# Attention: the scaled gate of tiles 1 to 14 is turned by VectorE in blocks and placed through memory, no longer by TensorE

## The reference, cut to what matters

```python
z = jnp.einsum('btd,dc->btc', x, w_in)
q, k, v, g_attn, hq, hf, hi, g_hg = jnp.split(z, _split_points(), axis=-1)
...
attn = _sink_window_attend(qb, k2, v2, qpos, kpos, sk).reshape(B, T, ATTN_WIDTH)
...
attn = _rmsnorm(attn, attn_g) * jax.nn.silu(g_attn.astype(jnp.float32))
...
mix = jnp.einsum('btc,cd->btd', jnp.concatenate([attn, o_hg], axis=-1), w_out.astype(jnp.float32))
```

## Time and profile before

| | us |
|---|---|
| median of three runs | 2558.17 |
| the profiled execution | 2546.3 |
| its span, first to last instruction | 2544.5 |
| PE busy in it | 2493.5 (98%) |
| DVE busy | 1705.2 (67%) |
| POOL busy | 1172.3 (46%) |
| ACT busy | 1113.5 (44%) |
| mean granted PE clock, share of full | 0.998 |

### The profile page before, as it was taken

One profiled execution on the slowest core, in us unless ns is written; L12 is line 12 of the kernel. 1 busy time (PEld: TensorE's weight loads), 2 busy tenths in 40 slices (PEclk: granted clock), 3 DMA queues, 4 the chain that ended last, 5 costly groups with the idle time before them and its releaser, 6 DMA issues. The chain is left out here.

```text
span 2544.5 us, 55195 instructions
## 1 busy us (share of the span) xinstructions
PE 2493.5 (98%) x20706; PEld 2044.3 (80%) x20706; DVE 1705.2 (67%) x3230; ACT 1113.5 (44%) x2542; POOL 1172.3 (46%) x1119
## 2 busy tenths in 40 slices
PE   8999989999999999999999999899999999999998
PEld 6788868888888788888888788688888887887887
DVE  5777777777676676654557777776777676866343
ACT  4455465555555510133334454555555554112322
POOL 2234315555556611496322443165555555116863
PEclk9999999999999999999999999999999999999999
DMA  5445552011110488765734555510111005877532
GB/s 182 154 172 185 187 186 70 27 43 43 44 38 25 175 288 293 273 216 172 264 123 154 186 179 178 190 35 31 43 43 51 31 33 195 313 270 257 170 135 91
DMA packets 176099, 365.44 MB, mean 144 GB/s; under 512 B 19104, under 2 KB 98464, under 8 KB 170272
## 3 DMA queue, kind: packets, MB, share of 16 engines
q1 hardware_dynamic: 175504, 363.11, 41.6%
q10 hardware_dynamic: 432, 0.08, 0.0%
HBM read 227.14 MB, written 137.89 MB: 143 GB/s over the span
## 5 line engine op out<-in xcount | busy, mean ns | idle before, releaser
L1947 PE MATMUL r_Z<-w_rec_parts,w_rec_xh 128*128 128x512 f32 x1920 | 610.3, 399 | 1.8 <-DVE r_kT L1768 0.9
L1947 PEld LDWEIGHTS r_Z<-w_rec_parts,w_rec_xh 128*128 128x128 f32 x1920 | 347.7, 188 | 71.9 <-issue 3.5
L1947 PE MATMUL r_Z<-w_rec_parts,w_rec_xl 128*128 128x512 f32 x960 | 375.7, 391 | 0.0
L124 PE MATMUL a_Z<-w_attn_high,w_attn_xh 128*128 128x512 f32 (+1 forms) x816 | 302.3, 370 | 11.6 <-DVE w_attn_low L211 9.7
L124 PE MATMUL a_Z<-w_attn_low,w_attn_xh 128*128 128x512 f32 (+1 forms) x816 | 290.6, 356 | 0.0
L124 PE MATMUL a_Z<-w_attn_high,w_attn_xl 128*128 128x512 f32 (+1 forms) x816 | 290.3, 356 | 0.0
L1649 ACT ACTIVATE r_E<-r_E 128x512 f32<-128x512 f32 x230 | 145.3, 632 | 294.6 <-DVE r_E L1805 292.1
L1540 POOL TENSOR_TENSOR r_qE<-r_qT,r_E 128x256 f32<-128x256 f32 x230 | 185.1, 805 | 190.6 <-ACT r_E L1649 115.4
L1947 PEld LDWEIGHTS r_Z<-w_rec_parts,w_rec_xl 128*128 128x128 f32 x960 | 180.2, 188 | 39.7
L1540 POOL TENSOR_TENSOR r_kE<-r_kT,r_E 128x256 f32<-128x256 f32 x230 | 201.2, 875 | 0.0
L124 PEld LDWEIGHTS a_Z<-w_attn_high,w_attn_xh 128*128 128x128 f32 x816 | 154.8, 190 | 39.9 <-issue 19.3
(11 more groups left out here) (338 smaller groups left out, 6409.3 us busy)
## 6 DMA issues: line engine op xcount, KB each, us to landing
dram_h_rows<-o_hb SPq DMA_DIRECT2D x34, 512.0 KB, 4.1
o_raw<-dram_hT SPq DMA_DIRECT2D x34, 512.0 KB, 4.3
o_hb<-dram_h_rows SPq DMA_DIRECT2D x34, 512.0 KB, 3.8
dram_y_all<-o_hb SPq DMA_DIRECT2D x34, 512.0 KB, 4.1
w_attn_xraw<-dram_xT SPq DMA_DIRECT2D x33, 512.0 KB, 5.7
w_rec_slot<-dram_w_in SPq DMA_DIRECT2D x16, 1024.0 KB, 8.2
o_mraw<-dram_mixT SPq DMA_DIRECT2D x32, 512.0 KB, 5.6
dram_hT<-o_hT SPq DMA_DIRECT2D x128, 128.0 KB, 2.6
```

What stands on the lines that cost most here:

```text
L124: mm = pe.matmul(out, a[:, c, :], b[:, c, :], start=(first and c == chunks[0] and a is xh and b is wh), stop=(last and c == chunks[-1] and ...
L1947: mm = pe.matmul(banks[what], x[:, c, :], w[:, cols[what]], start=(c == 0 and x is xh[k] and w is wh[c]), stop=(c == KC - 1 and x is xl[k]))
```

## The change

DVE no longer waits for PE with the gate. For tiles 1 to 14 `scale_gate` moves ahead of `row_max`; behind it a new `turn_gate` transposes `u` by blocks of 32x32 into `th`, the buffer of the gate's tanh. SP's new `store_gate` writes `th` to memory in four transfers (32 partitions each), and `load_gate_turned` reads it back into `attn`, now transposed as a whole. `gated` multiplies `attnT` by `attn` instead of by `T`, and it moves behind `unfold`. PE's `transpose_gate` goes from the step; `values` now waits for `ms_done` instead of `uT_out`. `gate_tanh` waits until the gate of two tiles earlier is back, since it writes `th`. Tiles 0, 15 and 16 keep the transposition on PE. The memory used is the one that the output phase writes later, and the semaphores of its transfers are renamed (`hT_st` to `turned_st`, `h_in` to `turned_in`); nothing else changes there.

```diff
@@ SP
+            def gate_home(n):
+                return dram["hT"][layer, n][:, 0:AW]
+
+            def store_gate(j, k):
+                n = 2 * j + k
+                sp.wait_ge(*S["turned"].at(n))
+                for i in range(4):
+                    sp.dma_start(gate_home(n).rearrange("(q r) (i x) -> i r q x", q=4, i=4)[i],
+                                 th[32 * i:32 * i + 32, :].rearrange("r (q x) -> r q x", q=4))                        .then_inc((S["turned_st0"], S["turned_st1"])[k].sem, 16)
+
+            def load_gate_turned(j, k):
+                n = 2 * j + k
+                sp.wait_ge(*(S["turned_st0"], S["turned_st1"])[k].at(64 * (j + k)))
+                sp.wait_ge(*S["uT_out"].at(n))
+                sp.dma_start(attn[:, :], gate_home(n)).then_inc(S["turned_in"].sem, 16)
...
             for j in range(1, PAIRS - 1):
                 c = 4 * (j - 1)
+                store_gate(j, 0)
                 exchange_part(c)
+                load_gate_turned(j, 0)
                 store_mix(j - 1, 1)
                 load_x(j + 2, 0)
                 exchange_part(c + 1)
                 store_mix(j, 0)
+                store_gate(j, 1)
                 exchange_part(c + 2)
+                load_gate_turned(j, 1)
@@ ACT, gate_tanh
                 wait(act, S["gate_done"], n)
+                if not isinstance(n, int) or n > 2:
+                    act.wait_ge(*S["turned_in"].at(16 * (n - 2)))
@@ DVE
             def scale_gate(j, k):
...
-                wait(dve, S["gT_ps"], n)
+                if isinstance(n, int) and n in (1, NT - 1):
+                    dve.wait_ge(*S["gT_ps"].at(1 if n == 1 else 2))
                 dve.tensor_scalar(u[:, :].rearrange("p (i s d) -> p s i d", s=KV, d=HD),
                                   gate[k][:, :].rearrange("p (s i d) -> p s i d", s=KV, d=HD), rstd[:, 0:1], None,
                                   ALU.mult).then_inc(S["scaled"].sem, 1)
 
+            def turn_gate(j, k):
+                n = 2 * j + k
+                dve.wait_ge(*S["scaled"].at(n + 1))
+                dve.transpose(th[:, :].rearrange("p (q i t) -> p q i t", q=4, i=4),
+                              u[:, :].rearrange("p (i q t) -> p q i t", q=4, i=4)).then_inc(S["turned"].sem, 1)
+
             def gated(j, k):
                 n = 2 * j + k
-                dve.wait_ge(*S["gT_ps"].at(n + 1))
+                if by_transfer(n):
+                    dve.wait_ge(*S["turned_in"].at(16 * n))
+                    wait(dve, S["attnT_done"], n)
+                    wait(dve, (S["mix_st0"], S["mix_st1"])[k], 64 * j)
+                    dve.tensor_tensor(in_tokens(mixT[k][:, :, :]), in_tokens(attnT[:, :, :]),
+                                      attn[:, :].rearrange("p (i c t) -> p c i t", i=4, c=4), ALU.mult)                        .then_inc(S["uT_out"].sem, 1)
+                    return
...
             def step(j, k, *chunks):
                 sum_squares(j - 1 + k, 1 - k)
+                scale_gate(j - 1 + k, 1 - k)
+                turn_gate(j - 1 + k, 1 - k)
                 row_max(j, k)
-                scale_gate(j - 1 + k, 1 - k)
                 for c in chunks[0:1]:
                     low_part(c, 2 * (1 - k))
                 divide(j, k)
                 rope(j + k, 1 - k)
+                unfold(j, k)
                 gated(j - 1 + k, 1 - k)
-                unfold(j, k)
                 gates(j + k, 1 - k)
@@ PE
             def values(j, k):
                 n = 2 * j + k
                 wait(pe, S["unfolded"], KV * n)
                 pe.wait_ge(*S["v_moved"].at(n + 1))
-                wait(pe, S["uT_out"], n)
+                if isinstance(n, int) and n in (1, NT - 1):
+                    pe.wait_ge(*S["uT_out"].at(n))
+                else:
+                    pe.wait_ge(*S["ms_done"].at(n))
...
                 score(j, k)
                 z_q(j + k, 1 - k)
-                transpose_gate(j - 1 + k, 1 - k)
                 z_g(j + k, 1 - k, 0)
```

More of the change, by code:

```diff
@@ L152 @@
     **counted(NT, "m_high m_split mix_ps summed stats_done var_done ve_done rstd_done scaled h_done"),
-    **counted(16 * NT, "m_in row_in h_in rows_in p_in"), "ln_in": 32, "weights_read": 2,
+    **counted(16 * NT, "m_in row_in turned_in rows_in p_in"), "ln_in": 32, "weights_read": 2,
     **counted(16 * (PAIRS + 1), "h_st0 y_st0"), **counted(16 * PAIRS, "h_st1 y_st1"),
-    **counted(64 * (PAIRS + 1), "hT_st0 yT_st0"), **counted(64 * PAIRS, "hT_st1 yT_st1"),
+    **counted(64 * (PAIRS + 1), "turned_st0 yT_st0"), **counted(64 * PAIRS, "turned_st1 yT_st1"),
     **counted(NT, "p_high p_split ple_ps blend y_done"), "turned": 2 * NT,
@@ L530, in attention_phase, with by_transfer @@
         own, before = slice(P, 2 * P), slice(0, P)
+        def by_transfer(n):
+            return not isinstance(n, int) or 1 <= n <= NT - 3
         part = [weights.beside[n][:, :] for n in ("part0", "part1")] + [kcT[:, :, :].rearrange("p b d -> p (b d)")]
@@ L651, in _ @@
             load_x(2, 1)
+            store_gate(0, 1)
+            load_gate_turned(0, 1)
             for j in range(1, PAIRS - 1):
                 c = 4 * (j - 1)
+                store_gate(j, 0)
                 exchange_part(c)
+                load_gate_turned(j, 0)
                 store_mix(j - 1, 1)
@@ L667, in _ @@
             store_mix(PAIRS - 2, 1)
+            store_gate(PAIRS - 1, 0)
+            load_gate_turned(PAIRS - 1, 0)
             sp.wait_ge(*S["z_g"].at(NT))
@@ L1035, in scale_gate @@
                                   ALU.mult).then_inc(S["scaled"].sem, 1)
+            def turn_gate(j, k):
[3 more added lines that the diff above has]
+                              u[:, :].rearrange("p (i q t) -> p q i t", q=4, i=4)).then_inc(S["turned"].sem, 1)
             def gated(j, k):
                 n = 2 * j + k
-                dve.wait_ge(*S["gT_ps"].at(n + 1))
+                if by_transfer(n):
[5 more added lines that the diff above has]
+                    return
+                dve.wait_ge(*S["gT_ps"].at(2 if n == NT - 2 else 3))
                 wait(dve, S["attnT_done"], n)
@@ L2205, in output_phase @@
         K = (slice(0, KC // 2), slice(KC // 2, KC))
-        h_st, hT_st = (S["h_st0"], S["h_st1"]), (S["hT_st0"], S["hT_st1"])
+        h_st, turned_st = (S["h_st0"], S["h_st1"]), (S["turned_st0"], S["turned_st1"])
         y_st, yT_st = (S["y_st0"], S["y_st1"]), (S["yT_st0"], S["yT_st1"])
@@ L2239, in store_h @@
                 for to, of in turned_to(th[0] if n == NT - 1 else hT[k], dram["hT"][layer, n]):
-                    sp.dma_start(to, of).then_inc(hT_st[k].sem, 16)
+                    sp.dma_start(to, of).then_inc(turned_st[k].sem, 16)
             def load_h(n, made):
                 k = n % 2
-                sp.wait_ge(*hT_st[k].at(64 * (n // 2 + 1)))
+                sp.wait_ge(*turned_st[k].at(64 * (n // 2 + 1)))
                 wait(sp, S["block_low"], made)
-                sp.dma_start(raw[k][:, :, :, :].rearrange("p i c t -> p (i c t)"), dram["hT"][layer, n]).then_inc(S["h_in"].sem, 16)
+                sp.dma_start(raw[k][:, :, :, :].rearrange("p i c t -> p (i c t)"), dram["hT"][layer, n]).then_inc(S["turned_in"].sem, 16)
             def load_rows(n, came):
@@ L2350, in add @@
                 if i == 0:
-                    pool.wait_ge(*S["h_in"].at(32 * q + 32))
+                    pool.wait_ge(*S["turned_in"].at(32 * q + 32))
                     wait(pool, S["block_low"], 7 * q)
@@ L2389, in _ @@
                 low_p(0, 2 * q + 1)
-            pool.wait_ge(*S["h_in"].at(16 * NT))
+            pool.wait_ge(*S["turned_in"].at(16 * NT))
             pool.wait_ge(*S["block_low"].at(7 * PAIRS))
@@ L2413, in high @@
                 if sums[k] is None:
-                    act.wait_ge(*S["h_in"].at(16 * NT if of is not None else 32 * q + 32))
+                    act.wait_ge(*S["turned_in"].at(16 * NT if of is not None else 32 * q + 32))
                     of = (b2, a1)[k - 1] if of is None else of
@@ L2465, in _ @@
             third(0)
-            act.wait_ge(*hT_st[1].at(64 * PAIRS))
+            act.wait_ge(*turned_st[1].at(64 * PAIRS))
             high_ps(0)
@@ L2549, in turn_h @@
                 dve.wait_ge(*S["h_done"].at(n + 1))
-                wait(dve, hT_st[k], 64 * (n // 2) if isinstance(n, int) else 32 * (n - k))
+                wait(dve, turned_st[k], 64 * (n // 2) if isinstance(n, int) else 32 * (n - k))
                 turn(th[0] if isinstance(n, int) and n == NT - 1 else hT[k], hb[k]).then_inc(S["turned"].sem, 1)
@@ L2567, in second_sum @@
                 if isinstance(q, int) and q == 0:
-                    dve.wait_ge(*hT_st[0].at(64 * PAIRS))
+                    dve.wait_ge(*turned_st[0].at(64 * PAIRS))
                 dve.tensor_tensor(r[:, :], X1, s[:, :], ALU.add).then_inc(S["recombined"].sem, 1)
@@ L2580, in corner @@
                 if k == 0 and isinstance(q, int) and q == 0:
-                    dve.wait_ge(*hT_st[0].at(64 * (PAIRS + 1)))
```

(1 more changed line is left out.)

4 lines of the change are left out of this document (2 added, 2 removed).

## The result

The changed kernel takes 2603.61 us (median of four runs, 2599.60 to 2608.58), the one before, run beside it, 2557.66 (2551.33 to 2558.35). The ratio is 1.0186, with a 95% interval of 1.016 to 1.0212: slower by some 47 us (41 to 54), where 2588.5 was forecast and 2566 to 2616 given as the range.

What follows compares the result with a forecast made beforehand. PE was taken to bound attention before the change; after it, PE waits for DVE and DVE for POOL. 31.7 + 1.5 - 1.2 - 1.7 = +30.3 us on 2558.2 gave 2588.5, range 2566 to 2616 for 8 in 10.

Steps and rivals of the forecast that it cites:

- The hold: DVE's moved scaling starts just after POOL's split_low and is held 2.20 us by it, bounds 0 to 2.39.
- The cycle: Attention steps of tiles 3 to 14, from one values to the next: 20.62 us instead of 19.30.
- The rule of the ports: DVE's scaling, a two-port operation, waits for all of POOL's split_low, let in 0.19 us before its record ends.
- The transposition: DVE's new 128x512 transposition of the gate takes 0.71 us, bounds 0.487 and 1.246.
- The step of tile 2: This step has no low_part and ACT's exponentials decide: 0.75 us more, 1.5 for both layers.
- The late load: The turned gate's load through memory was taken as in time, at no cost; coming late had chance 0.08.
- point of decision: The load's time from issue to landing, 6.1 us, beyond which gated would be late and lengthen steps.
- The cover: SP issues the gate's load some 5.2 us before gated wants it, plus 0.9 us of slack.
- The way: The gate's 256 KB load back from memory, judged by a 512 KB load that lands in 4.3 us.
- second rival: The gate comes back late, each us beyond 6 counting in 26 steps: 2615 with 7 us; chance 0.08.
- The ends of the layers: In tile 15's step the scaling is hidden and gated behind unfold saves 0.6 us, 1.2 for both layers.
- PE's gain: Dropping PE's four transpositions saves 0.44 us a step, 12.3 us in 28 steps if nothing else becomes late.

Runs made afterwards that it cites:

- e5: Kernel before, with only DVE's scaling of the gate moved ahead of row_max; PE still turns the gate: 2585.15 us, 1.0107.
- e6: Kernel before, with the scaling ahead of row_max and POOL's split_low waiting for the scaling: 2558.87 us, 1.001.
- e1: Changed kernel, with POOL's split_low waiting for DVE's scaling of the gate: 2562.34 us, 1.0021.
- e9: Changed kernel, with POOL's split_low waiting for the scaling and ACT issuing the turned gate's load behind its exponentials: 2556.14 us, 0.9996.
- e8: Changed kernel, with POOL's split_low waiting for the scaling and SP issuing the gate's load between the exchange's stores and the next part's load: 2555.32 us, 0.9995.
- e2: Changed kernel, with SP issuing the turned gate's load ahead of the exchange of weights: 2605.23 us, 1.0192.
- e13: e9 with ACT also issuing the four stores of the turned gate, ahead of its exponentials: 2557.44 us, 1.0.
- e7: Kernel before, without PE's four transpositions in the steps of tiles 2 to 15, leaving the gate of tiles 1 to 14 unturned: 2549.43 us, 0.9972.

## Why the prediction was right, and where it was off

**The hold: right.** Where it was said to come from, how long (2.60 us, in 26 of 28 steps), and that it sets the cycle. The cycle was put at 20.62 us; ten of the 24 steps of tiles 3 to 14 lie between 20.57 and 20.67. e5 gives 27.4 us for the move without the transposition, e6 takes it back, e1 takes 41 us off the changed kernel.

**The rule of the ports: agrees, with a margin.** The Trainium skill ("SBUF — State Buffer", section "SBUF: two separate sides") says that of a VectorE operation with two ports or two inputs and a GpSimd operation, whichever starts first has the shared ports for its whole instruction. In the rows 0.06 us were enough to lose them, and they came free 0.2 us ahead of the end of POOL's record.

**The transposition: right.** 0.711 us, taken as 0.71. The 0.53 us taken off for half the columns doesn't follow from the large one, though, of which half is 0.62; only the bounds were worked out from rows.

**The step of tile 2: right.** Forecast +1.5 us for both layers, measured (19.89 + 20.18) - 2 x 19.30 = +1.5.

**The late load: wrong, and the largest error.** The step was "I take it as in time", with a point of decision at 6.1 us and a chance of 0.08. Both sizes in it were off. The cover: in half of the steps SP issues the load of the next part between the two stores and the gate's load. The forecast doesn't name it, and it leaves 3.8 to 4.2 us until `gated` wants the gate, not 5.2. The way: behind these 1.5 MB the load takes 5.2 to 7.4 us; the row of 4.3 us came from the output phase, where other transfers stand ahead. By the point of decision of 6.1 us only two of the 28 loads would have been late, and `gated` waits in 17 steps. The 24 steps sum to 506.4 us, where 24 x 20.62 = 494.9 was forecast: +11.5 us. Ten of them are longer than 20.9, and in eight of these PE waits for the row sums, 0.27 to 2.25 us.

How much of it is the load's? e5 has the same hold and no way through memory. Its 24 steps sum to 492.9 us, 13.5 less, and its undisturbed ones are 20.45 and 20.54 us long in the two layers instead of 20.58 and 20.66; that difference, for the transposition and the new order, makes 3 us in 24 steps. About 10 us are left for the way through memory. They aren't all `gated`'s wait, since in e9 weights that land late lengthen the same steps. With the hold gone, e8 against e1 puts the load's place at 1.0021 - 0.9995 = 0.26%, some 7 us (1 to 12 by the two intervals). So forecast and second rival were true together, not one or the other: the hold in 26 of 28 steps, and on top the late load, which lengthens fewer than half. That the time stayed within the range is owed to the width that this rival had been given.

**The ends of the layers: wrong sign.** For tile 15 a saving of 1.2 us was forecast, and tile 16 unchanged. Tile 15's two steps are together 1.2 longer (43.90 instead of 42.68), tile 16's 2.2 (38.25 instead of 36.08): 4.6 us off. In tile 15's step the mean square comes 0.9 us later after `values` in layer 0 and 0.7 in layer 1. That is the late `gated`: in e2, whose gate is in time, it comes as before, and the two steps take 42.11 us. In layer 0 ACT also gets the input of the recurrence later, 6.16 us after the mean square instead of 5.35; in layer 1 it is 5.73 instead of 5.68. The new entries in SP's queue alone don't explain that: in e13 they are gone, and it is 6.39 and 6.73. Tile 16's two steps take 36.6 to 37.0 us in e5, e6 and e7, and 37.2 to 38.5 in every run with the way through memory; why stays open.

**PE's gain: mis-sized.** 0.44 us a step was forecast. Where nothing else holds PE (e1, e8, e9) it is 19.30 - 18.81 = 0.49. In e7, with `gated` still ahead of `unfold`, DVE's chain takes back part of it, as the distance of 0.42 us between DVE's end and PE suggests, and tile 15's step doesn't shrink at all (21.25 and 21.62 against 21.16 and 21.52): 7.2 us of the 12.3. It changed nothing in the forecast, in which PE waits anyway.

**Sum.** Steps of tiles 3 to 14 +41.5 (forecast 31.7 - 1.7 = 30.0), tile 2 +1.5 (+1.5), tiles 15 and 16 +3.4 (-1.2): +46.3 against +30.3. The median of the runs moved by 45.9.

Open: why e8, e9 and e13 stop near 1.000 and not at e7's 0.9972 or below. Tiles 3 to 14 take 461.5 us in e9, 456.9 in e7 and 464.9 in the kernel before. Five more transfers a step and weights that land late are in their rows. What of it is SP's order, what the shared way to memory, e13 didn't part, since ACT's issues cost what SP's order gave back.

## What to carry to other kernels

Before an elementwise operation on SBUF is moved on VectorE, look at what GpSimd does in the new place; beside a long GpSimd instruction even 0.49 us can cost 2.1 in every step. If the early place is wanted, try letting GpSimd wait for VectorE; here that gave the loss back. A round trip through memory is only as fast as the traffic ahead of it: price it from what is issued right ahead of it, on whichever queue, and not from the same tensor in a calmer phase. And count its cover from the moment of its own issue, with every issue that stands in between.
